# Inference step of a hybrid decoder on one core: in the projections stage, a unit's exponentials one step later on ScalarE, its last products and its stores at the beginning of the next unit

## The reference

```
xn = rms_norm(x, p['norm_mix'])
proj = xn @ p['w_in']
q = rope(proj[..., :NSA_WIDTH]...)            # and the keys; the values are kept as they are
xm = p_rw + (prev - p_rw) * p['rw_mu']        # p_rw: the RWKV columns, prev: the row before
r, wa, k, v, aa, ga = jnp.split(xm, ...)
w = -softplus(-(rw_w0 + tanh(wa) @ rw_w_b)) - 0.5
decay = exp(-exp(w))
a = sigmoid(rw_a0 + aa @ rw_a_b)
kk = (k * rw_k_k) / norm of it per head
k_h = k * (1 + (a - 1) * k_a)
```

## Time and profile before

| | |
|---|---|
| median of 3 runs | 4350.12 us (4350.04 to 4350.73) |
| the profiled execution, its time | 4343.49 us |
| its span | 4341.7 us |
| TensorE busy | 4019.6 us, 93% |
| VectorE busy | 2207.7 us, 51% |
| ScalarE busy | 1119.1 us, 26% |
| GpSimd busy | 1785.8 us, 41% |
| granted clock of TensorE, mean | 0.952 |

### The profile page before, as it was taken

One profiled execution on the slowest core, in us unless ns is written; L12 is line 12 of the kernel. 1 busy time (PEld: TensorE's weight loads), 2 busy tenths in 40 slices (PEclk: granted clock), 3 DMA queues, 4 the chain that ended last, 5 costly groups with the idle time before them and its releaser, 6 DMA issues. The chain is left out here.

```text
span 4341.7 us, 89511 instructions
## 1 busy us (share of the span) xinstructions
PE 4019.6 (93%) x37002; PEld 3657.7 (84%) x37002; DVE 2207.7 (51%) x4923; ACT 1119.1 (26%) x2467; POOL 1785.8 (41%) x2332
## 2 busy tenths in 40 slices
PE   8988899988799999999999888999788999999997
PEld 8977788865569999999898777888655799999996
DVE  6676544348754423424456764444587544244153
ACT  3243233226561000000212432333365510001011
POOL 5523221127665444434354322221277644444342
PEclk9988999988999999999999889999799999999998
DMA  3244422220013122131323443222200131321312
GB/s 130 86 144 149 113 80 68 74 94 6 11 30 121 46 89 86 44 117 52 110 83 103 131 153 100 77 80 66 89 6 12 59 101 44 102 69 47 129 40 87
DMA packets 201960, 350.42 MB, mean 81 GB/s; under 512 B 72930, under 2 KB 135650, under 8 KB 200418
## 3 DMA queue, kind: packets, MB, share of 16 engines
q1 hardware_dynamic: 201554, 344.70, 25.4%
HBM read 253.44 MB, written 95.90 MB: 80 GB/s over the span
## 5 line engine op out<-in xcount | busy, mean ns | idle before, releaser
L2580 POOL CAST wr_hi<-wr_raw 128x256 fp32r<-128x256 f32 x584 | 263.6, 451 | 904.2 <-PE ps L2615 898.5
L2582 POOL TENSOR_TENSOR wr_lo<-wr_raw,wr_hi 128x256 fp32r<-128x256 f32 x584 | 547.9, 938 | 46.7
L2615 PE MATMUL ps<-xh,wr_hi 128*128 128x384 f32 x2064 | 453.6, 328 | 0.0
L2615 PE MATMUL ps<-xh,wr_lo 128*128 128x384 f32 x2064 | 453.1, 327 | 0.0
L2615 PE MATMUL ps<-xl,wr_hi 128*128 128x384 f32 x2064 | 453.0, 327 | 0.0
L1356 POOL TENSOR_TENSOR rc_CT<-rc_AT,rc_masks 128x256 f32<-128x256 f32 x192 | 138.1, 738 | 661.9 <-DVE rc_AT L1391 484.6
L2615 PEld LDWEIGHTS ps<-xh,wr_hi 128*128 128x128 f32 x2064 | 348.9, 188 | 0.3
L2615 PEld LDWEIGHTS ps<-xl,wr_hi 128*128 128x128 f32 x2064 | 348.9, 188 | 0.0
L2615 PEld LDWEIGHTS ps<-xh,wr_lo 128*128 128x128 f32 x2064 | 348.8, 188 | 0.0
L2653 ACT ACTIVATE de_c<-de_c 128x1088 f32<-128x1088 f32 (+1 forms) x44 | 49.1, 1115 | 1098.2 <-DVE de_c L2740 1098.2
L2615 PE MATMUL ps<-de_mixh,wr_hi 128*128 128x384 f32 (+3 forms) x1440 | 321.0, 331 | 7.9 <-DVE de_mixl L2687 7.9
(11 more groups left out here) (450 smaller groups left out, 8418.9 us busy)
## 6 DMA issues: line engine op xcount, KB each, us to landing
sa_kvp<-in_cache SPq DMA_DIRECT2D x128, 256.0 KB
scr_xres<-de_x SPq DMA_DIRECT2D x56, 544.0 KB, 2.7
de_x<-scr_xres SPq DMA_DIRECT2D x56, 544.0 KB, 3.7
wr_raw<-in_w_gate SPq DMA_DIRECT2D x42, 512.0 KB, 3.5
wr_raw<-in_w_up SPq DMA_DIRECT2D x42, 512.0 KB, 3.5
rc_arbk<-scr_arbk SPq DMA_DIRECT2D x32, 512.0 KB, 4.7
wr_raw<-in_w_down SPq DMA_DIRECT2D x32, 512.0 KB, 3.6
pr_raw<-in_w_rw SPq DMA_DIRECT2D x28, 512.0 KB, 4.4
```

Of the source, the lines that this page charges most:

```text
L2580: pool.tensor_copy(hi[:, k, :], raw[:, k, :]).then_inc(w_hi, 1)
L2582: pool.tensor_tensor(lo[:, k, :], raw[:, k, :], f32(hi[:, k, :]), ALU.subtract).then_inc(w_ready, 1)
L2615: m = pe.matmul(ps[:, (bank + b) * BANK:(bank + b) * BANK + cols], w[rows, k, :], x[rows, k, o:o + cols], start=(k == 0 and i == 0), stop= ...
```

## The change

Of each unit three things move. ScalarE's exponentials go from piece 1 to piece 2, so that one more of its attention steps stands ahead of them. VectorE's last operations of a unit, the copies to `wend` and the two products of kk * a with the inverse decay, go from the end of piece 3 to the beginning of piece 0 of the next unit, which puts a rotation ahead of them. The stores go from the end of piece 3 to piece 1 of the next unit, and the store of `rk` now stands ahead of that of `arbk`. The last unit keeps both in its own piece 3. Nothing is added or left out.

```
@@ -339,6 +339,15 @@
+        def store_unit(sp, n):
+            hp, grp = UNITS[n]
+            o, w = GROUPS[grp]
+            c = o // CH
+            sp.wait_ge(pool_out, 2 * n + 2)
+            sp.dma_start(X["rk"][hp, :, o:o + w], f_rk[:, 0:w]).then_inc(rk_kept, 16)
+            sp.wait_ge(out_ready, n + 1)
+            sp.dma_start(X["arbk"][c:c + w // CH, :, hp].rearrange("c p n -> p c n"), f_out[:, 0:w // CH].rearrange("p c a t -> p c (a t)")).then_inc(f_kept, 16)
...
@@ -374,13 +383,12 @@
                         sp.wait_ge(pool_out, 2 * n)
                     load_unit(sp, n + 1)
                 yield
-                yield
-                yield
-                sp.wait_ge(out_ready, n + 1)
-                sp.wait_ge(pool_out, 2 * n + 2)
-                c = o // CH
-                sp.dma_start(X["arbk"][c:c + w // CH, :, hp].rearrange("c p n -> p c n"), f_out[:, 0:w // CH].rearrange("p c a t -> p c (a t)")).then_inc(f_kept, 16)
-                sp.dma_start(X["rk"][hp, :, o:o + w], f_rk[:, 0:w]).then_inc(rk_kept, 16)
+                if n:
+                    store_unit(sp, n - 1)
+                yield
+                yield
+                if n + 1 == len(UNITS):
+                    store_unit(sp, n)
                 yield
...
@@ -655,7 +664,6 @@
                 act.activation(f_wi[:, 0:w], f_cum[:, 0:w], ACT.Exp, scale=E05).then_inc(decays, 1)
                 act.wait_ge(prev_ready, n + 1)
                 act.activation(f_pw[:, 0:w], f_sw[:, 0:w], ACT.Exp, scale=-E05).then_inc(decays, 1)
-                yield
                 yield
                 yield
 
...
         def features_vector(dve):
+            def removals(n):
+                hp, grp = UNITS[n]
+                o, w = GROUPS[grp]
+                c = w // CH
+
+                def parts(x):
...
+                if grp < 2:
+                    dve.tensor_copy(wend[:, hp, 6 * grp:6 * grp + 6], f_w[:, CH - 1:w:CH])
+                else:
+                    dve.tensor_copy(wend[:, hp, 12:NCH], f_w[:, CH - 1:256:CH])
+                    dve.tensor_copy(wend[:, hp, NCH:NCH + NB], f_w[:, 256 + NQ - 1:w:NQ])
+                dve.wait_ge(kka_ready, n + 1)
+                for e in range(2):
+                    hf = slice(64 * e, 64 * e + 64)
+                    m = dve.tensor_tensor(f_out[hf, 0:c, 2 + e, :], parts(f_kk[n % 2])[hf], parts(f_wi)[hf], ALU.mult)
+                m.then_inc(out_ready, 1)
+
...
+                if n:
+                    removals(n - 1)
                 yield
                 dve.wait_ge(gates_ready, 2 * n + 1)
                 dve.tensor_tensor_scan(f_cum[:, 0:w], zero, f_sw[:, 0:w], 0.0, ALU.mult, ALU.add).then_inc(cum_ready, 1)
...
                 dve.tensor_tensor(kk, kk, a, ALU.mult).then_inc(kka_ready, 1)
-                if grp < 2:
-                    dve.tensor_copy(wend[:, hp, 6 * grp:6 * grp + 6], f_w[:, CH - 1:w:CH])
-                else:
-                    dve.tensor_copy(wend[:, hp, 12:NCH], f_w[:, CH - 1:256:CH])
-                    dve.tensor_copy(wend[:, hp, NCH:NCH + NB], f_w[:, 256 + NQ - 1:w:NQ])
-                dve.wait_ge(kka_ready, n + 1)
-                for e in range(2):
-                    hf = slice(64 * e, 64 * e + 64)
-                    m = dve.tensor_tensor(f_out[hf, 0:c, 2 + e, :], parts(kk)[hf], parts(f_wi)[hf], ALU.mult)
-                m.then_inc(out_ready, 1)
+                if n + 1 == len(UNITS):
+                    removals(n)
                 yield
```

More of the change, by code:

```diff
@@ L728, in features_vector @@
         def features_vector(dve):
+            def removals(n):
[3 more added lines that the diff above has]
+                def parts(x):
+                    return x[:, 0:w].rearrange("p (c t) -> p c t", t=CH)
+                if grp < 2:
[8 more added lines that the diff above has]
+                m.then_inc(out_ready, 1)
             for n, (hp, grp) in enumerate(UNITS):
```

## The result

The changed kernel takes 4287.11 us, the median of 4 runs (4283.56 to 4296.14). The kernel before, with one more run beside them, takes 4350.08 us (4347.58 to 4350.73). The ratio is 0.986, with a 95% interval of 0.9848 to 0.9871: 63 us or 1.4% faster, where 4288 was forecast.

What follows compares the result with a forecast made beforehand. TensorE, busy 93% of the span, was the bound: 160 + 7.1 + 6.0 = 173.1 us a stretch; with 2.8 us at each end, gains of 30.4 and 31.9, together 62: 4350.1 to 4288 us, range 4264 to 4328.

Steps and rivals of the forecast that it cites:

- The bound and TensorE's own need: In each layer's stretch of attention columns beside RWKV units, TensorE needs 160 us; some 41 us are lost to waits and clock.
- The ring: ScalarE and VectorE waiting on each other from unit to unit: about 15 us before, 11.6 after, 12.9 with gates.
- ScalarE's wait at the exponentials: Sign in the changed profile: this wait, up to 7.5 us before, would be short.
- What remains: Losses left in each stretch: waits of 3.6 and 2.5 us, each with 3.5 us of lower clock; 173.1 us in all.
- The end: From the last step's matmuls to the end of unit 11's products, 2.8 us before: gain 2.8 us, nothing at the least.
- The rotation behind the key factor: Sign: VectorE's rotation there, 2.86 us beside GpSimd's products, would take near 1 us in units without splitting.
- The stores: Two DMAs a unit, issued later by about a rotation and 1.27 us, would cost nothing.
- a margin: Time between a unit's store landing and VectorE needing it to have landed in the next unit: 2 us.
- Copies and products: Moved behind a rotation on VectorE: nothing for the ring, one rotation 1.27 us earlier, mattering only where GpSimd slows the block.
- The exponentials: One piece later on ScalarE: 1.92 us leave the ring, and overlap with GpSimd's products falls from 1.9 to about 0.4 us.

Runs made afterwards that it cites:

- e4: The changed kernel with the exponentials one piece later still, in piece 3: 4288.43 us.
- e5: The changed kernel with GpSimd splitting only 8 of 256 columns in the last two groups of attention columns, most queries left uncomputed: 4272.83 us.
- e3: The changed kernel with both stores back at the end of piece 3: 4315.49 us.
- e1: The kernel before with only the exponentials moved to piece 2; products and stores in their old place: 4319.31 us.
- e8: The kernel before with exponentials and stores moved as in the change, copies and products left at the end of piece 3: 4300.39 us.
- e10: The kernel before with only the stores moved, to piece 1 of the next unit: 4342.55 us.
- e7: The changed kernel with the stores one piece later still, in piece 2 of the next unit: 4297.05 us.
- e9: The kernel before with only the exponentials moved, and five buffers for the rotated rows instead of three: 4289.52 us.
- e6: The changed kernel with GpSimd's splitting pieces and their loads every second attention step instead of every step: 4284.31 us.

## Why the prediction was right, and where it was not

- **The bound and TensorE's own need: right.** I took 160 us. After: 174.5 less 7.8 of waits, less 4% of 174.5 for the clock (7.0), is 159.7; in the second layer 175.3 less 10.3 less 3% (5.3) is 159.7 too.
- **The ring: right in its terms.** The one unit that shows it takes 11.54 us where the terms give 11.47; that this is also near the 11.6 of the prediction, meant for four steps without gates, is chance. That TensorE sets the pace most of the time is read from ScalarE's waits for it (30.6 us at L629 alone) and fits e4. ScalarE's wait at the exponentials isn't as short as I said, up to 5.0 us in eight units, and VectorE still waits up to 2.4 us for what stands behind them.
- **What remains: right in sum.** I put 7.1 + 6.0 = 13.1 us a layer, 173.1 for a stretch; it is 174.5 and 175.3. Of that waits were 6.1 and clock 7.0; they are 7.8 and 7.0 in the first layer, 10.3 and 5.3 in the second. The longest wait, forecast 3.6 us beside weight splitting, measured 3.7 and 3.9 just there. e5 shows the splitting as the cause of the 3.9, not of the 3.7.
- **The end: right.** 2.8 us forecast, 3.9 and 3.5 measured in the two layers. The products are done 0.6 us before TensorE is (368.06 and 368.70), and the next stage begins 4.3 us behind them where it was 4.8.
- **The rotation behind the key factor: right in quiet units only.** At 295.66 it takes 0.94 us with GpSimd's products already over (293.57 to 295.55). With splitting it takes 3.5 us and more. The Trainium skill, "SBUF — State Buffer", section "Who interferes with whom", was cited for work that is cheap or dear by what GpSimd does at its new place. The trace agrees: in unit 1 GpSimd's product began at 225.16, 2.0 us behind the key factor since it waited for the landing, and the pair of L790 at 225.24 took 2.63 us beside it where it takes 1.11 in a quiet unit. In the mean L790 went from 788 to 814 ns and the moved products (L773, now L753) from 552 to 639, too little to take much back.
- **The stores: the step that failed.** The prediction said: "The sync engine was held at the end of every unit; now it isn't", and went on to a margin and "cost nothing". It looked only for what the later store might cost and never asked who had been waiting behind the earlier one. It was ScalarE, for the landing of stored rows, a wait that my description of its step in the kernel before left out (the order rows name it, `kv_kept`), and that the prediction named only for rows behind the new store. The runs give 28 us to it (e3 against the change), 19 us where the products stay (e1 against e8) and 5 us where the exponentials stay (e10). The cost was about right: VectorE never waits for the store in the change, GpSimd starts at most 2.2 us later for it (up to 3 was said), and one piece more costs 10 us (e7).
- **Copies and products: mis-sized.** "costs and gives the ring nothing" is true of the ring, and the condition behind it, "this only matters where GpSimd slows the block", is where the 13 us of e8 come from, by the one place looked at. I named the condition and priced it at nothing. The price depends on the rest: with the stores in their old place it is 4 us, within the noise (e1 against e3), and with five buffers the kernel is as fast without the move (e9).
- **The exponentials: credited with everything.** Alone they bring 28 of the 63 us. The single parts, 28.2 for the exponentials and 12.5 for the rest, add up to 41; the other 22 exist only together, since each part ends a wait that hides behind another's.

The total came out right because I had worked it out from the far side: TensorE's need plus what I thought must remain. That sum doesn't need the parts. It assumed that no further wait stood behind the ring; one did, the queue, and the change happened to remove it. So the time came out by luck in this part: the cause named for it, the exponentials, brings less than half. Had only the exponentials been moved, the same argument would have said 4290 to 4303, as the expectation of e1 did, and the kernel took 4319.

Open: what part of e7's 10 us comes from GpSimd's late start and what from VectorE's one wait, and whether spreading the splitting is worth anything (e6).

## What to carry to other kernels

When a long wait goes away, ask of each engine's queue what else was late at that time: two waits that lie on top of each other show only the one that ends last, and the trace of before had 3.4 us of ScalarE's waits under the name of the landing and 6.1 us under "issue", where e1 had 19.7 and 24.3. An in-order DMA queue that waits for the end of a job holds every store behind it, and the price is paid by whoever needs those buffers back; moving the waiting store back and adding buffers each did it here. A sum made from the bounding engine's need gave a good total for this change, but it said nothing of which part earns it.

## What the runs showed of the hardware

**The clock falls behind some waits and not others.** Windows of the changed kernel behind three waits of TensorE: of 1.45 us (until 284.25), of 2.47 us (until 316.09), and of 3.68 us (until 239.81; the third line of the windows at the top).

```profile
284.60:290.60 6.00, 5.89 (x40) 4.99 (x40) 5.86 (x21) 1.22 (x5) 0.00 (x0) 1.00 0.71 212
316.50:323.50 7.00, 7.00 (x30) 6.14 (x30) 6.67 (x18) 3.07 (x6) 2.02 (x3) 0.51 0.33 114
```

The first stays at 2.4 GHz; the second runs its 7 us at 0.51, that is 1.2 GHz; the longest wait is followed by a mean of 0.64, about 5 us at the lower level and the rest at the higher. The wait of 2.5 us thus cost another 3.4 here, and the one of 1.45 us nothing. The window in the earlier trace rows, behind a wait of 3.3 us, had the same 0.51. But the length of the wait alone doesn't decide: in e7, behind a wait of 2.51 us (until 322.75) at the same place, the clock stays up,

```profile
323.10:330.10 7.00, 7.00 (x55) 6.50 (x54) 6.76 (x18) 3.07 (x6) 2.09 (x2) 1.00 0.33 114
```

and in e8 the 7 us behind a wait of 1.29 us (until 295.16) have a mean of 0.76. What decides is open.

**Small VectorE operations suffer most beside GpSimd.** An operation of the rotation with 128x64 elements takes 0.22 us alone, and this beside the splitting:

```profile
280.85 1.32 DVE L729 TENSOR_TENSOR pr_tb<-pr_kvt,pr_cs 128x64 f32<-128x64 f32 x1
282.09 0.63 DVE L730 TENSOR_TENSOR pr_tb<-pr_kvt,pr_cs 128x64 f32<-128x64 f32 x1
282.75 1.31 DVE L732 TENSOR_TENSOR pr_kvt<-pr_tb 128x64 f32<-128x64 f32 x1
```

1.32 us is about one operation of GpSimd (L465, 1.30 us, began at 280.79): the small one gets through when that is over. The larger pair (L790) takes 2.63 for 1.11.

**A run-to-run spread of 12 to 22 us.** The changed kernel's four runs lie 12.6 us apart (0.3%). The four of before beside them lie within 3.2, but the 39 beside the experiments reach from 4337.2 to 4359.7 (0.5%). Differences of a few microseconds between medians of four or five runs, as those of e4 and e6 to the change, are not told from nothing.
